# Hybrid SSD / RG-LRU layer: dt's softplus by token with sums on TensorE, no GpSimd work, output projection in two halves

## The chip, the cores and the metric

One core of a Trainium2 chip runs the whole program. The metric is the device time of one execution in microseconds. Lower is better.

## The reference

A decoder trunk of two layers on x (256 tokens, width 1024), all in float32. Each layer is a half-weighted SwiGLU FFN (width 2816), a mixer, and a second FFN. The mixer of layer 0, the hybrid, is what the change touches:

```python
z, xbc, dt_raw, gate_b, x_b = split(rms_norm(h) @ w_in)       # 1024, 1536, 16, 1024, 1024
xbc = silu(causal_dwconv(xbc)); xa, B, C = split(xbc)         # 16 heads of 64; 2 groups, state 128
dt = softplus(dt_raw + dt_bias); a = -exp(a_log)
cs = cumsum(dt * a) in chunks of 128                          # per head
y = (C B^T * exp(cs_i - cs_j), causal) @ (xa * dt)  (+ the carry of chunk 0)  + d * xa
y_a = rms_norm(y * silu(z), in two groups of 512)
xb = causal_dwconv(x_b); r, i = sigmoid(xb @ w_ra), sigmoid(xb @ w_ix)   # 16 blocks of 64
a_t = exp(-8 * r * softplus(-lambda)); h_t = a_t * h_(t-1) + sqrt(1 - a_t^2) * i * xb
y_b = gelu(gate_b) * h_t
h = h + concat(y_a, y_b) @ w_out                              # 2048 x 1024
```

## The kernel before

**Layout.** Everything is held feature-major: 128 features on the partitions, 256 tokens along the row. A float32 weight block of 1024 x 128 is split into a rounded high part (`whi`, ScalarE, L185) and the rest (`wlo`, VectorE, L190), the activations likewise (`xn`, `hid`), and a block is 24 matmuls: high by high and high by low for each of 8 tiles (L201, L202), then low by high (L205). Blocks go through a ring of four slots; SyncE loads a slot once the low part of the block four before is made, and ScalarE makes a high part once TensorE is through with the block four before.

**Phases.** FFN, hybrid, FFN, FFN, attention, FFN. In the hybrid, two blocks are a "pair": 18 pairs of the input projection (pairs 0 to 5 conv tiles of xbc, 6 to 9 of the LRU's input, 10 to 13 z, 14 to 17 gates), then 16 blocks of the output projection.

**Order.** Each engine has an order written out by hand. TensorE (`hyb_tensor`, L764) multiplies pair j and then does what `after[j]` lists: dt's product, `c_dot_b`, transposes of x to tokens (`x_to_tokens`, L795), the heads' products (`head_y`, L807/L808), the LRU's gate products (`lru_gates`, L820/L821), the group sums (one-column matmuls, L830) and their spread (L840). Before pair j it waits until pair j-2 is read out of PSUM. ScalarE (`hyb_scalar`) and VectorE (`hyb_vector`) run a loop over s: VectorE reads pair s-2 (`read_pair`, L1016), multiplies decays by C B^T (`decay_products`, L1118), makes exponents (`exponents`, L1112), makes the low parts of pair s (`convert_lo`, L190), and then does `todo[s]`, with the conv's taps of pair s-2 (L1028) last or nearly so. ScalarE makes the high parts of pair s and then does its own `todo[s]`. For pairs 15 and 16 VectorE makes the second high part too (L257).

**What the change touches.** dt's softplus is done on rows of 16 heads by 256 tokens: `softplus_args`, `softplus_u`, `softplus_ratio`, `steps_of_dt` on VectorE, `softplus_exp` and `softplus_ln` on ScalarE, then `sums_of_dt`, two scans on VectorE (L1078); TensorE turns the results into token-major columns (`rows_to_tokens`, L776), which VectorE copies to `tok`. The scanned rows `cs` also go to DRAM and come back spread over the partitions (`csb`, L751 to L756). lambda's softplus (128x8) goes along with it. GpSimd does `lru_ix` (L1252), a 128x1024 product, and `gate_y` (L1259, L1261), a product and a square of 128x512 for each two tiles. `lru_mult2`, `mult_of_lru`, `lru_scan`, `gelu`, `lru_out`, `lru_hi` and `lru_lo` make the recurrent half of `hid` (tiles 8 to 15) in steps 17 to 19 and just behind; `y_norm`, `y_hi`, `y_lo` the SSD half (tiles 0 to 7) in steps 18 and 19. `OUT_BLOCKS` (L719) orders the output blocks (tile d, half q), almost tile by tile; `out_tile` adds a finished tile to `h` and makes the next phase's input of it. The FFN before the hybrid has down pairs e = 0 to 7 with `down_out` (L614, L616) and `residual_hi` (L292).

## Time and profile before

| what | us |
|---|---|
| median of 3 runs (1081.31 to 1082.31) | 1081.52 |
| the profiled execution | 1081.11 |
| its span, first to last instruction | 1079.3 |
| TensorE busy in the span | 1054.2 |
| hybrid phase: first matmul to the next phase's first | 195.84 to 395.86 |

The profile is of one execution, and its times count from the span's start. PE is TensorE's matmuls, PEld its weight loads, DVE VectorE, ACT ScalarE, POOL GpSimd, SP SyncE. "Granted clock" is the share of 2.4 GHz that TensorE was allowed: 1.00, or 0.50, which is 1.2 GHz. Durations of neighbouring instructions overlap a little, so the time from start to start is what an instruction costs its engine.

### The profile page before, as it was taken

Reading aid. Unit: us, or ns where it says so; the run is one execution under the profiler, and the core shown is the slowest. Engines: PE = TensorE matmul, PEld = TensorE weight load, DVE = VectorE, ACT = ScalarE, POOL = GpSimd, SP = SyncE. Lnnn points to the kernel's source line nnn. Section 1 sums busy time; section 2 is a strip of 40 time slices with the busy share of each in tenths; the row PEclk is TensorE's granted clock in tenths of the full one; section 3 lists DMA queues with packets and bytes.
Section 4 is the critical chain, followed back from the end, with each engine's and each line's share of the span. In section 5 each row is a group of like instructions: output and inputs, shape, how many; then the busy total and the mean of one; then the engine's idle time right before and its main releaser. Section 6 shows DMA issues by size and latency. Waiting matters only on the chain. (4 is left out here: it accounts for less than half of the span.)

```text
span 1079.3 us, 18474 instructions
## 1 busy us (share of the span) xinstructions
PE 1054.2 (98%) x6669; PEld 949.0 (88%) x6669; DVE 807.9 (75%) x1141; ACT 614.2 (57%) x982; POOL 69.2 (6%) x80
## 2 busy tenths in 40 slices
PE   9999999998988999999999999999999999999997
PEld 8888888897888998888888888888989998888886
DVE  6888775799898758888656888766689578888753
ACT  6555543676887555555534555544455756555541
POOL 0200011100131000000011000002100000000021
PEclk9999999998988999999999999999999999999999
DMA  9866676556443656667764666775475437666671
GB/s 253 215 192 190 197 215 170 141 152 204 117 123 102 178 160 191 194 193 209 195 189 142 190 190 191 222 195 166 120 203 158 126 100 213 192 189 196 190 206 39
DMA packets 365602, 189.07 MB, mean 175 GB/s; under 512 B 5840, under 2 KB 364512, under 8 KB 365552
## 3 DMA queue, kind: packets, MB, share of 16 engines
q1 hardware_dynamic: 365296, 187.84, 61.6%
q0 software_dynamic: 256, 0.59, 0.3%
q8 instruction: 29, 0.48, 0.2%
q14 instruction: 21, 0.17, 0.1%
HBM read 186.81 MB, written 1.06 MB: 174 GB/s over the span
## 5 line engine op out<-in xcount | busy, mean ns | idle before, releaser
L190 DVE TENSOR_TENSOR wlo<-raw,whi 128x1024 fp32r<-128x1024 f32 (+1 forms) x324 | 419.8, 1315 | 67.9 <-ACT whi L185 66.3
L185 ACT ACTIVATE whi<-raw 128x1024 fp32r<-128x1024 f32 (+1 forms) x322 | 352.1, 1114 | 26.5 <-PE psum L205 19.9
L217 PE MATMUL psum<-xn,whi 128*128 128x512 f32 x1408 | 354.4, 393 | 0.1
L217 PEld LDWEIGHTS psum<-xn,whi 128*128 128x128 f32 x1408 | 253.5, 189 | 45.9 <-DVE xn L302 0.4
L220 PEld LDWEIGHTS psum<-xn,wlo 128*128 128x128 f32 x1408 | 192.4, 190 | 13.8
L220 PE MATMUL psum<-xn,wlo 128*128 128x256 f32 x1408 | 196.9, 282 | 0.0
L217 PE MATMUL psum<-hid,whi 128*128 128x512 f32 x704 | 171.8, 391 | 0.0
L217 PEld LDWEIGHTS psum<-hid,whi 128*128 128x128 f32 x704 | 128.1, 189 | 24.0
L201 PE MATMUL psum<-xn,whi 128*128 128x256 f32 x480 | 124.1, 295 | 0.7 <-ACT arena L1530 0.7
L202 PE MATMUL psum<-xn,whi 128*128 128x256 f32 x480 | 121.2, 288 | 0.0
L505 ACT ACTIVATE arena<-arena 128x256 f32<-128x256 f32 x88 | 36.9, 420 | 112.1 <-DVE arena L558 112.1
L201 PEld LDWEIGHTS psum<-xn,whi 128*128 128x128 f32 x480 | 94.8, 198 | 4.5 <-issue 3.2
L220 PEld LDWEIGHTS psum<-hid,wlo 128*128 128x128 f32 x704 | 92.9, 191 | 4.9
L202 PEld LDWEIGHTS psum<-xn,whi 128*128 128x128 f32 x480 | 94.8, 198 | 0.1
L220 PE MATMUL psum<-hid,wlo 128*128 128x256 f32 x704 | 94.4, 282 | 0.0
L292 ACT ACTIVATE xn<-h,vec 128x256 fp32r<-128x256 f32 x48 | 23.7, 506 | 116.4 <-DVE h L616 101.3
L509 ACT ACTIVATE hid<-arena 128x256 fp32r<-128x256 f32 x88 | 36.9, 419 | 88.6 <-DVE arena L563 88.6
L568 DVE TENSOR_TENSOR hid<-arena,hid 128x256 f32 (+1 forms) x88 | 37.5, 426 | 60.0 <-ACT hid L509 60.0
L205 PE MATMUL psum<-xn,wlo 128*128 128x256 f32 x480 | 68.4, 285 | 0.0
L558 DVE TENSOR_TENSOR arena<-arena,rb 128x512 f32<-128x512 f32 x88 | 60.9, 693 | 3.1
L205 PEld LDWEIGHTS psum<-xn,wlo 128*128 128x128 f32 x480 | 63.0, 195 | 0.0
L554 DVE TENSOR_TENSOR arena<-psum,arena 128x512 f32<-128x512 f32 x88 | 60.2, 684 | 3.5 <-ACT arena L500 3.5
(218 smaller groups left out, 913.6 us busy)
## 6 DMA issues: line engine op xcount, KB each, us to landing
raw<-in_ffn_gate SPq DMA_DIRECT2D x88, 512.0 KB, 3.9
raw<-in_ffn_up SPq DMA_DIRECT2D x88, 512.0 KB, 3.9
raw<-in_ffn_down SPq DMA_DIRECT2D x64, 704.0 KB, 4.6
raw<-in_hyb_w_in SPq DMA_DIRECT2D x36, 512.0 KB, 4.3
raw<-in_dif_w_qkv SPq DMA_DIRECT2D x24, 512.0 KB, 4.6
raw<-in_hyb_w_out SPq DMA_DIRECT2D x16, 512.0 KB, 4.3
raw<-in_dif_w_o SPq DMA_DIRECT2D x8, 512.0 KB, 4.3
hid<-cs_rows SPq DMA_DIRECT2D x4, 512.0 KB, 6.7
```

Source lines behind the costliest of these rows:

```text
L185: act.activation(whi[:, s, 0:k * P], raw[:, s, 0:k * P], ACT.Copy).then_inc(s_whi, 1)
L190: dve.tensor_tensor(wlo[:, s, 0:k * P], raw[:, s, 0:k * P], whi[:, s, 0:k * P].bitcast(F32), ALU.subtract).then_inc(s_wlo, 1)
L201: pe.matmul(acc, hi[:, j, :], x[:, t, 0, :], start=start and j == 0, stop=False)
L202: pe.matmul(acc, hi[:, j, :], x[:, t, 1, :], start=False, stop=False)
L205: mm = pe.matmul(acc, lo[:, j, :], x[:, k0 + j, 0, :], start=False, stop=stop and j == k - 1)
L217: pe.matmul(acc, hi[:, j, :], x[:, t, :, :], start=start and j == 0, stop=False)
L220: mm = pe.matmul(acc[:, T:2 * T], lo[:, j, :], x[:, k0 + j, 0, :], start=False, stop=stop and j == k - 1)
L505: act.activation(act_g[:, g, :], gu[:, g, 0, :], ACT.Silu).then_inc(s_silu, 1)
L509: act.activation(hid[:, bass.ds(j, 1), 0, :].rearrange("p a t -> p (a t)"), hu[:, g, :], ACT.Copy).then_inc(s_hhi, 1)
L554: dve.tensor_tensor(gu[:, g, :, :], wide_parts(g)[0], cor[:, g, :, :], ALU.add).then_inc(s_gu, 1)
L558: dve.tensor_tensor(gu[:, g, :, :], gu[:, g, :, :], rb2, ALU.mult).then_inc(s_gn, 1)
L568: dve.tensor_tensor(v[:, 1, :], hu[:, g, :], v[:, 0, :].bitcast(F32), ALU.subtract).then_inc(s_hlo, 1)
```

## The change

dt is transposed to tokens first, and softplus is done there on 128x32; the running sums are made by TensorE as products with a triangle of ones, once as rows (for `cs`) and once by token (for `tok`), and ScalarE copies them out. lambda's softplus moves into the down pairs of the FFN before. GpSimd's work moves: products to VectorE, squares to ScalarE. The masks of C B^T become one instruction for the four diagonal blocks, and ScalarE copies the other two. `x_to_tokens` uses four PSUM banks. The output projection does all eight tiles of the SSD half first, each in a bank of its own, then the recurrent half, which VectorE and ScalarE make in steps 19 to 21. The core of the diff:

```diff
 # FFN before the hybrid, ScalarE, after convert_hi of down pair e
+                    if e == 3: lambda_exp_of_lru(act)
+                    elif e == 4: lambda_ln_of_lru(act)
 # the same, VectorE, after convert_lo
+                    if e == 2: lambda_args(dve)
+                    elif e == 4: lambda_u(dve)
+                    elif e == 5: lambda_value_of_lru(dve)
...
-        OUT_BLOCKS = [(0, 0), (1, 0), (0, 1), (1, 1)] + [(d, q) for d in range(2, DT) for q in range(2)]
+        OUT_BLOCKS = [(d, q) for q in range(2) for d in range(DT)]
+        def out_sum(d):
+            return banks[(5, 7, 6, 4, 0, 1, 2, 3)[d]][:, 0:T]
-        CB_BANK = (6, 2)
+        XT_BANK = (4, 2, 5, 7)
...
 # TensorE
+            def dt_to_tokens():
+                pe.wait_ge(s_dtx, 1)
+                for c in range(TC):
+                    mm = pe.transpose(dt_tok[:, c * HEADS:(c + 1) * HEADS], dt_rows[:, c * P:(c + 1) * P],
+                                      ident[0:HEADS, 0:HEADS])
+                mm.then_inc(s_dtt, 1)
+            def sums_of_dt():
+                pe.wait_ge(s_sp, 10)
+                for c in range(TC):
+                    pe.matmul(sum_rows[:, c * P:(c + 1) * P], DTA[:, c * HEADS:(c + 1) * HEADS], tri, start=True, stop=True)
+                pe.matmul(sum_tok[:, 0:2 * HEADS], tri, DTN, start=True, stop=True)
+                pe.matmul(sum_tok[:, 2 * HEADS:], tri, DTN[:, 0:HEADS], start=True, stop=False)
+                pe.matmul(sum_tok[:, 2 * HEADS:], ones, DTA[:, 0:HEADS], start=False, stop=True).then_inc(s_sums, 1)
-            after[0] += [dt_product]
-            after[5] += [c_dot_b]
-            after[6] += [rows_to_tokens]
-            for g, s in enumerate((6, 7, 7, 8)):
+            after[0] += [dt_product, rows_of_heads]
+            after[2] += [dt_to_tokens]
+            after[5] += [sums_of_dt, c_dot_b]
+            for g, s in enumerate((6, 7, 8, 9)):
                 after[s] += [lambda g=g: x_to_tokens(g)]
-            after[14] += [lambda: group_sums(0)]
+            after[15] += [lambda: group_sums(0)]
...
 # ScalarE
+            def take_sums():
+                act.wait_ge(s_sums, 1)
+                act.activation(cs, sum_rows, ACT.Copy).then_inc(s_cs, 1)
+                act.activation(tok[:, 2 * HEADS:], sum_tok, ACT.Copy).then_inc(s_tok, 1)
+            def square_y(k):
+                act.wait_ge(s_yg, k + 1)
+                act.activation(sz[:, 2 * k:2 * k + 2, :], xbc[:, 2 * k:2 * k + 2, :], ACT.Square).then_inc(s_ysq, 1)
+            todo[3] += [softplus_exp]
+            todo[4] += [softplus_ln]
+            todo[6] += [take_sums, take_cb_off]
             for j in range(6):
-                todo[j + 3] += [lambda j=j: conv_silu(j)]
+                todo[max(j + 3, 4)] += [lambda j=j: conv_silu(j)]
-            todo[2] += [softplus_exp]
-            todo[3] += [softplus_ln]
-            todo[17] += [lambda: gelu(0), lambda: group_rms(0)]
-            todo[18] += [lambda: group_rms(1), lambda: mult_of_lru(1), lambda: gelu(1)]
-            todo[18] += [lambda: lru_hi(0)] + [lambda t=t: y_hi(t) for t in range(4)]
+            todo[15] += [lambda: square_y(0), lambda: square_y(1)]
+            todo[17] += [lambda: square_y(2), lambda: square_y(3), lambda: group_rms(0)]
+            todo[18] += [lambda: group_rms(1)] + [lambda t=t: y_hi(t) for t in range(4)]
             todo[19] += [lambda t=t: y_hi(t) for t in range(4, 8)]
-            todo[19] += [lambda: lru_hi(1), lambda: gelu(2), lambda: gelu(3)]
+            todo[19] += [lambda: mult_of_lru(1), lambda: gelu(0), lambda: gelu(1)]
+            todo[20] += [lambda: gelu(2), lambda: gelu(3), lambda: lru_hi(0), lambda: lru_hi(1)]
+            todo[21] += [lambda: lru_hi(2), lambda: lru_hi(3)]
...
 # VectorE
             def softplus_args():
+                dve.wait_ge(s_dtt, 1)
+                dve.wait_ge(s_arow, 1)
+                dve.tensor_copy(D_[:, 0:HEADS], head_rows[:, 0:HEADS]).then_inc(s_hrow, 1)
+                dve.wait_ge(s_hrow, 2)
+                dve.tensor_tensor(by_head(X_), by_head(dt_tok), D_[:, 0:HEADS].unsqueeze(1).to_broadcast([P, TC, HEADS]),
+                                  ALU.add).then_inc(s_spx, 1)
...
-            for g, s in enumerate((8, 9, 9, 10)):
+            for g, s in enumerate((8, 9, 10, 11)):
                 todo[s] += [lambda g=g: take_x(g)]
+            todo[13] += [lambda: lru_ix(0), lambda: lru_mult2(0)]
+            todo[14] += [lambda: gate_y(0), lambda: gate_y(1)]
+            todo[16] += [lambda: gate_y(2)]
+            todo[17] += [lambda: gate_y(3), lambda: y_rrms(0)]
+            todo[18] += [lambda: y_norm(0), lambda: y_rrms(1)] + [lambda t=t: y_lo(t) for t in range(4)]
+            todo[19] += [lambda: lru_ix(1), lambda: lru_mult2(1)]
+            todo[20] += [lambda: lru_scan(1), lambda: lru_out(0), lambda: lru_out(1)]
+            todo[21] += [lambda: lru_out(2), lambda: lru_out(3)] + [lambda k=k: lru_lo(k) for k in range(4)]
+            for d in range(4):
+                todo[24 + d // 2] += [lambda d=d: out_tile(d)]
+            small_work = {2: scaled_dt, 3: softplus_args, 4: softplus_u, 5: steps_of_dt}
-            for s in range(20):
+            for s in range(26):
...
-                if s == 8:
-                    take_tok()
+                if s in small_work:
+                    small_work[s]()
```

`steps_of_dt` now holds the ratio and the end of the softplus and the two products with a. In the loop `small_work` stands after `read_pair` and `decay_products` and ahead of `exponents` and `convert_lo`. The last out tiles (4 to 7) are left to the start of the next phase.

## Rows read from the trace of the kernel before

**Rows 1.** The page's first part: busy us, share of the span, instructions.

```profile
PE 1054.2 (98%) x6669; PEld 949.0 (88%) x6669; DVE 807.9 (75%) x1141; ACT 614.2 (57%) x982; POOL 69.2 (6%) x80
```

**Rows 2.** Windows of the hybrid: stretch, length, busy per engine, granted clock, DMA, GB/s.

```profile
195.80:347.40 151.60, 139.60 (x1045) 131.70 (x1044) 137.08 (x221) 113.11 (x190) 19.69 (x12) 0.93 0.51 143
347.40:395.90 48.50, 47.14 (x391) 46.83 (x391) 31.72 (x52) 25.13 (x41) 0.00 (x0) 1.00 0.54 156
```

**Rows 3.** TensorE's waits in the hybrid: us in total, times, longest.

```profile
PE psum L795 <- DVE arena L1100: 4.9, 1, 4.9
PE psum L807 <- DVE arena L1123: 4.7, 2, 2.6
PE psum L840 <- DVE small L1165: 1.6, 1, 1.6
```

**Rows 4.** Windows beside two of the holes, columns as in the second group.

```profile
303.20:306.60 3.40, 1.27 (x11) 1.08 (x10) 3.40 (x4) 3.37 (x6) 0.66 (x1) 1.00 0.10 19
306.60:310.10 3.50, 3.49 (x13) 2.71 (x14) 2.72 (x5) 2.91 (x6) 0.00 (x0) 0.51 0.99 274
337.40:344.20 6.80, 6.80 (x33) 6.80 (x33) 6.46 (x12) 4.39 (x9) 0.00 (x0) 0.50 0.54 157
```

**Rows 5.** Timeline of VectorE, steps 3 to 11: start, us, instruction, idle before.

```profile
211.74 0.69 DVE L1016 TENSOR_TENSOR arena<-psum,rb 128x512 f32<-128x512 f32 x1 [1.11 <-PE psum L205]
212.35 2.35 DVE L190 TENSOR_TENSOR wlo<-raw,whi 128x1024 fp32r<-128x1024 f32 x2
...
221.54 0.41 DVE L1055 TENSOR_TENSOR arena<-arena 16x256 f32<-16x256 f32 x1
221.99 1.74 DVE L1056 RECIPROCAL arena<-arena 16x256 f32<-16x256 f32 x1
223.77 2.46 DVE L1028 SCALAR_TENSOR_TENSOR arena<-arena,vec 128x256 f32<-128x256 f32 x6
...
247.14 0.17 DVE L1053 TENSOR_SCALAR small<-small 128x8 f32<-128x8 f32 x1
...
271.75 0.69 DVE L1016 TENSOR_TENSOR arena<-psum,rb 128x512 f32<-128x512 f32 x1
```

**Rows 6.** Timeline of VectorE, later: exponents, low parts, scans, tiles' low parts.

```profile
257.46 0.75 DVE L1112 SCALAR_TENSOR_TENSOR arena<-small,hid 128x256 f32<-128x256 f32 x2
...
300.27 2.69 DVE L1112 SCALAR_TENSOR_TENSOR arena<-small,hid 128x256 f32<-128x256 f32 x2
302.88 3.19 DVE L190 TENSOR_TENSOR wlo<-raw,whi 128x1024 fp32r<-128x1024 f32 x2
...
313.64 2.44 DVE L1141 TENSOR_TENSOR_SCAN arena<-arena 128x256 f32<-128x256 f32 x4
...
349.89 1.42 DVE L1177 TENSOR_TENSOR hid<-arena,hid 128x256 fp32r<-128x256 f32 x4
```

**Rows 7.** Timeline of ScalarE, steps 11 to 19.

```profile
273.68 0.40 ACT L913 ACTIVATE arena<-arena,small 128x128 f32<-128x128 f32 x1 [2.92 <-DVE arena L1112]
...
292.05 1.99 ACT L185 ACTIVATE whi<-raw 128x1024 fp32r<-128x1024 f32 x2
...
316.16 1.28 ACT L922 ACT_TABLE_LOAD   x1 [2.74 <-DVE arena L1141]
...
341.00 1.28 ACT L946 ACT_TABLE_LOAD   x1
342.30 0.64 ACT L946 ACTIVATE arena<-arena 128x512 f32<-128x512 f32 x1
```

**Rows 8.** Timeline of TensorE: the first group's sums, and the next phase's first matmuls.

```profile
320.24 1.84 PE L830 MATMUL psum<-con,arena 128*128 128x1 f32 x16
...
395.86 1.55 PE L217 MATMUL psum<-xn,whi 128*128 128x512 f32 x6
```

**Rows 9.** Waits of the whole execution, columns as in the third group.

```profile
ACT xn L292 <- DVE h L616: 101.3, 24, 5.3
DVE h L614 <- PE psum L220: 53.8, 24, 6.8
```

More of the change, by code:

```diff
@@ new lines, in lambda_args, with lambda_exp_of_lru, lambda_u @@
+        def lambda_args(dve):
+            dve.wait_ge(s_vec, 16)
+            dve.tensor_scalar(lt[0], vec[:, VEC["lru_lambda"]:VEC["lru_lambda"] + NL], -1.0, None,
+                              ALU.mult).then_inc(s_lmx, 1)
+        def lambda_exp_of_lru(act):
+            act.wait_ge(s_lmx, 1)
+            act.activation(lt[1], lt[0], ACT.Abs).then_inc(s_lme, 1)
+            act.wait_ge(s_lme, 1)
+            act.activation(lt[1], lt[1], ACT.Exp, scale=-1.0).then_inc(s_lme, 1)
+        def lambda_u(dve):
+            dve.wait_ge(s_lme, 2)
+            dve.tensor_scalar(lt[2], lt[1], 1.0, None, ALU.add).then_inc(s_lmu, 1)
@@ L872, in hyb_tensor @@
             for k, (d, q) in enumerate(OUT_BLOCKS):
-                if q == 0:
-                    read_out(pe, p0 + 16 + d)
+                if q == 0 and d in (4, 5):
+                    read_out(pe, p0 + 12 + d)
                 b = 2 * (p0 + 18) + k
-                multiply(pe, b, b % RING, DT, hid, 8 * q, half(p0 + 18 + d, 0), start=q == 0, stop=q == 1,
+                multiply(pe, b, b % RING, DT, hid, 8 * q, out_sum(d), start=q == 0, stop=q == 1,
                          need=ready if d == 0 else None)
@@ L993, in hyb_scalar @@
                     task()
-            for k in (2, 3):
-                lru_hi(k)
-            for s in range(20, 26):
-                convert_hi(act, p0 + s, DT)
-                residual_hi(act, n + 1, s - 20)
-            return [lambda: residual_hi(act, n + 1, DT - 2), lambda: residual_hi(act, n + 1, DT - 1)]
+            return [lambda: [residual_hi(act, n + 1, d) for d in (4, 5, 6)], lambda: residual_hi(act, n + 1, 7)]
         nlam8 = small[:, 138:146]
@@ L1124, in take_y, with lru_ix, gate_y @@
                                          ALU.add).then_inc(s_yr, 1)
+            def lru_ix(k):
+                dve.wait_ge(s_gs, 8 * k + 8)
+                dve.tensor_tensor(li[:, :, :], li[:, :, :], lxb(k), ALU.mult).then_inc(s_ix, 1)
+            def gate_y(k):
+                dve.wait_ge(s_sz, k // 2 + 1)
+                dve.wait_ge(s_yr, 2 * k + 2)
+                y = xbc[:, 2 * k:2 * k + 2, :]
+                dve.tensor_tensor(y, y, sz[:, 2 * k:2 * k + 2, :], ALU.mult).then_inc(s_yg, 1)
             def lru_mult2(k):
@@ L1178, in y_lo, with out_tile @@
                                   ALU.subtract).then_inc(s_ylo, 1)
-            todo = {s: [] for s in range(20)}
-            todo[0] += [dt_weights]
-            todo[2] += [softplus_args]
-            todo[3] += [softplus_u]
-            todo[4] += [lambda: softplus_ratio(U_, D_, M_)]
-            todo[5] += [steps_of_dt]
-            todo[6] += [sums_of_dt]
-            todo[7] += [lambda: take_cb(0), lambda: take_cb(1)]
-            for g, s in enumerate((8, 9, 9, 10)):
+            def out_tile(d):
+                dve.wait_ge(s_blk, 2 * (p0 + 18) + OUT_BLOCKS.index((d, 1)) + 1)
+                add_residual(dve, n, d, out_sum(d), 1.0)
+                residual_lo(dve, n + 1, d)
+            todo = {s: [] for s in range(26)}
+            todo[0] += [dt_weights, diagonals_of_heads]
+            todo[7] += [take_cb]
+            for g, s in enumerate((8, 9, 10, 11)):
                 todo[s] += [lambda g=g: take_x(g)]
@@ L1192, in hyb_vector @@
                 todo[10 + m] += [lambda m=m: take_y(m)]
-            todo[13] += [lambda: lru_mult2(0)]
-            todo[17] += [lambda: lru_mult2(1), lambda: lru_out(0), lambda: y_rrms(0)]
-            todo[18] += [lambda: y_norm(0), lambda: y_rrms(1), lambda: lru_scan(1), lambda: lru_out(1)]
-            todo[18] += [lambda: lru_lo(0)] + [lambda t=t: y_lo(t) for t in range(4)]
-            todo[19] += [lambda: lru_lo(1)]
+            todo[13] += [lambda: lru_ix(0), lambda: lru_mult2(0)]
[6 more added lines that the diff above has]
+            todo[21] += [lambda: lru_out(2), lambda: lru_out(3)] + [lambda k=k: lru_lo(k) for k in range(4)]
+            for d in range(4):
+                todo[24 + d // 2] += [lambda d=d: out_tile(d)]
             for j in range(10):
                 todo[j + 2] += [lambda j=j: conv_taps(j)]
-            todo[7] += [scale_of_lambda]
+            small_work = {2: scaled_dt, 3: softplus_args, 4: softplus_u, 5: steps_of_dt}
             def read_pair(j):
@@ L1208, in read_pair @@
                     gate_scaled(j - 14)
-            for s in range(20):
+            for s in range(26):
                 if s == 0:
                     before[0]()
-                if s >= 2:
+                if 2 <= s < 20:
                     read_pair(s - 2)
```

222 lines of the change are left out of this document (121 added, 101 removed).

## The prediction

> **What bounds the kernel now.** I first read the page's busy line: TensorE is busy 98% of the span [rows 1], so elsewhere there is little to win. Then the windows of the hybrid stage, up to and after the end of its 18 input pairs: 12.0 us of the first 151.6 us are idle on TensorE and its mean clock is 0.93; the output projection loses 1.4 us and keeps its clock [rows 2]. The stage ends with the first FFN matmul at 395.86 [rows 8]. TensorE's waits name the holes: 4.9 us for the take of x (L1100, itself held behind VectorE's queue), 4.7 us for `take_y` (L1123), 1.6 us for the group scale [rows 3]; with the 1.4 of the projection [rows 2] that is 12.6 us. The windows beside the holes show a second price: after 3.4 us of which TensorE was idle for 2.1, before 306.6, the clock is 0.51 for the next 3.5, and after the hole before L840 it is 0.50 for 6.8 [rows 4]. That is 1.2 GHz in place of 2.4, and half such a stretch is lost: 1.7 and 3.4 us. So over 12 us of holes and some 10 us of clock (0.07 of 151.6) are at stake. These holes all wait for VectorE, so the question is what VectorE and, through it, ScalarE still have ahead of each release.
>
> I call what VectorE and ScalarE do in the loop's round s "step s". In it VectorE reads pair s-2 and makes the low parts for pair s, which TensorE multiplies next. Prices, start to start, from VectorE's rows: read 0.61, two low parts 2.27, six taps 2.38, two exponents 0.67; a 128x512 operation 0.61, a 128x1024 one 1.13, so the 128x768 of `decay_products` 0.86; a low part of one tile 0.34, `take_y`, which also reads PSUM, 0.39 [rows 5, 6]. A pair is 48 matmuls at 0.12, 5.76 us; a block of the output projection is 2.88.
>
> **1. dt's chain (steps 2 to 7).** Removed from VectorE: 0.4 to 1.74 us operations on 16x256 (the reciprocal is 1.74 [rows 5]), two scans, three of the four `take_cb` operations, lambda's chain; together some 7 us. Added: ten operations of 128x32, bounded by 0.17 (128x8) and 0.41 (16x256), the reciprocal by 0.2 and 1.74 [rows 5]; I take 0.21 each and 0.38 for the reciprocal, near the short row since 32 is near 8: 2.3 us. But three waits come with it.
> - Step 3: the new `softplus_args` waits for the transposes that TensorE makes behind pair 2, and it stands ahead of step 3's low parts. VectorE begins step 3 when pair 1 ends, at 211.74 [rows 5]; pair 2 ends 5.76 later at 217.5, the transposes take 0.2, so its low parts begin at 218.2, where they began at 212.35. This 5.8 us is the price. TensorE barely feels it (first low part at 219.4, wanted 1.92 us into pair 3, at 219.6).
> - Step 4: ScalarE has the Ln and its reload, two `conv_silu` and their reload ahead of `conv_first`; the taps wait about 1.1 us.
> - Step 5: the ten operations stand ahead of the low parts, and pair 5 waits about 1.5 us. Step 6: `take_sums` and `take_cb_off` wait for TensorE ahead of `conv_first(4)`: 1.6 us for the taps.
>
> Steps 3 to 7 then start at 212.0, 222.9, 229.5, 237.0, 243.9; step 8 at 249.8, step 9 at 256.6, step 10 at 264.0, step 11 at 271.8. Before, step 11 started at 271.75 [rows 5]. **The 7 us saved are spent on the waits, and the gain up to step 11 is nil.** The 4.9 us hole at L795 goes, and what is late next is `take_y(0)` (VectorE at 269.4; TensorE arrives at 265.5): a new hole of about 4 us one pair later. TensorE gains 0.8 us of small matmuls (sums 0.8, two spreads 0.4, less 0.4 removed; near the 0.11 a 128-column pass takes), all of it within these holes.
>
> **2. Steps 11 to 13.** ScalarE runs without a pause from its decays at 273.68, which waited for step 11's exponents, through its reloads to the high parts of pair 13 at 292.05 [rows 7]. The start hangs on the same VectorE step, so it is equal: high part 293.1, two low parts 295.4, `take_y(3)` 295.8. That hole, one of the two at L807, stays.
>
> **3. GpSimd left out.** While GpSimd ran, the two exponents took 2.69 in place of 0.75 and the two low parts 3.19 in place of 2.35 [rows 6]. Moved to VectorE: two 128x1024 products (1.25 with their wait) and four of 128x512 (0.61); to ScalarE: four squares of 128x512 at 0.54 (the Gelu row of that shape, 0.64 busy [rows 7]). Steps 13 to 15 on VectorE: `lru_ix` 297.05; two products 299.45; read, decay, exponents 301.6; low parts 303.85; `take_y(4)` 304.3; two `gate_y` 305.45. TensorE arrives at `head_y(10)` at 304.4, where it then stood still until 306.6 [rows 4]; this hole closes, and pair 14 starts 2.65 later (two heads, four gate products, at full clock), at 307.05. Step 15: 0.61 + 0.86 + 0.67 + 3.0 (low, cast, low) = 310.6, scan 1.25 + 2.36 = 314.2, `take_y(5)` 314.7. TensorE now waits for it from 312.95: a new hole of 1.85, and 0.75 for the sigmoids behind the scan (ScalarE waits for it [rows 7]). Pair 15 starts at 318.15.
>
> Then ScalarE: sigmoids 316.95, squares 318.05, high part 319.1, sigmoids 320.5, a reload and eight lru activations 4.65 to 325.15, high parts 327.15, squares as `gate_y(3)` allows (329.5) to 330.1, reload, `group_rms(0)` 331.65, early enough for TensorE, which ends pair 16 at 332.45. The hole of 1.6 at L840 goes. Pair 17 starts at 332.45 + 0.45 + 1.75 (L830 [rows 8]) = 334.65 and ends at **340.5; before it was 347.4, where rows 2 are cut. Gain 6.9**: holes 4.5 less 2.6, clock 1.7 and 3.4.
>
> **4. The output projection.** Its total is unchanged (16 x 2.88). The first block's wait is the same chain as before (read, `y_norm`, `y_lo` of 4 tiles 1.42 [rows 6]): it ends at 345.2. But the recurrent half is now made behind it, by two engines that wait for each other: low parts 19 to 346.4; `lru_ix`, `lru_mult2` to 350.1; Sqrt 351.1; reload 1.3 and two Gelu 353.45; high parts 354.5 and 355.5; low 356.8; scan 360.4; two `lru_out` 361.6; `lru_hi(1)` 362.35; and only then ScalarE makes the high part of the seventh block: 363.4. TensorE wants the fifth at 353.85 (waits 0.65) and the seventh at 360.3 (**waits 3.15**). Blocks 7 and 8 to 369.2, the recurrent tiles are then ready (369.65, before their last one is wanted), eight blocks to 392.25. A hole of 3.15 will drop the clock, as those of 2.1 and 2.6 did: +1.7, so **393.95** against 395.86. The out tiles' residuals have 5.76 us for 5 us of work on VectorE; what ends the stage is the last tile, as before.
>
> In this part a rule speaks against the change. A reload here is 1.28 us, and the Gelu behind it starts 1.30 after it [rows 7]. The Trainium skill (ScalarE: Activation LUTs, "What ACT_TABLE_LOAD costs") gives about 1.38 us of drain beside it, 2.66 in all; by that the stage would end 1.4 us later and the gain be 0.5. The row shows no such drain, and no term here rests on it.
>
> **5. Lambda in the FFN before.** Two more reloads and four small activations on ScalarE lie in its waits for L616, 4.2 us in each down pair (101.3 by 24); on VectorE 2.1 us of 128x8 operations in one step stand beside waits of 2.2 for TensorE (53.8 by 24) [rows 9], and any rest is within the one pair's lead of the low parts. Cost nil; without that cover 0.4 us. The SyncE queue: `cs` is ready at 239.3, about 1.4 us later than before, behind weight loads which are later anyway; a broadcast that lands late for step 8 is bounded by these 1.4, and step 8 starts later too. I take nothing.
>
> **Sum.** Nil to step 11, 6.9 to the end of pair 17, then 3.3 lost in waits and 1.7 in clock: 1.9 to 2.0. The profiled execution took 1081.11 (span 1079.3); the median of the runs is 1081.52, 0.4 above it, and the difference is applied to that: **1079.5**. About 0.2% (2.2 us) is what a measurement can tell from no change, so my forecast lies on that edge.
>
> **Rivals.**
> (a) *The early chain is shorter than I think.* If ScalarE comes to `conv_first` in time in steps 4 and 6, VectorE is 2.7 earlier at step 11, and so are ScalarE's chain and everything behind it; if the waits in the output projection are also too short for the clock, 1.7 more: 1075.1. For it: the 128x32 durations are estimates. Against: each wait is an order of instructions, read in the code.
> (b) *The clock turns the gain round (slower).* New pauses lie at the ends of pairs 14 (1.85 + 0.75) and 16 (spread and sums, 2.2 us of one-column matmuls), where the clock of before fell after 2.1 idle, and for 6.8 us after 1.6 idle followed by such sums [rows 3, 4]. If they cost 1.7 and 3.4, pair 17 ends at 345.6, and the chain of part 4 hangs from that end, unshortened: 1079.5 + 5.1 = 1084.6. It decides once more than 2.0 is lost so. Against: after the same sums at 320.24, with no long hole ahead of them, the clock stayed [rows 8].
> (c) *An even result.* Step 3's wait is passed on worse than I count (a reload in front of a waiting Exp or Ln adds 1.3 on VectorE), the gain of part 3 is eaten, 1081.5.
> (d) *The slow VectorE rows were not GpSimd's doing.* Then steps 14 and 15 keep 2.8 us: 1082.3. Against: the exponents take 0.75 whenever GpSimd is still.
>
> **Numbers.** Forecast 0.50 (own range 1077.5 to 1081.5; of it 0.24 faster by over 0.2%, 0.26 within), (a) 0.20, (b) 0.16, (c) 0.10, (d) 0.04, of which half within. Faster 0.44, same 0.38, slower 0.18. Range 1074.8 to 1085.0, from (a) to (b).
>
> **What would show it.** Step 3 of VectorE: its low parts begin at about 218, after a wait for TensorE of 5 to 6 us; step 11 begins within 1 us of 271.8. No wait of L795's kind, one of about 4 us for the first `take_y`. No VectorE exponents above 0.8. Pair 17 ends near 340.5. One hole of about 3 us at the seventh output block, which waits for its high part. First FFN matmul after the stage near 394. Wrong if step 11 begins 3 us earlier, or if the seventh block finds its high part ready.

## The result, and the profile after

| what | before | changed |
|---|---|---|
| median, us | 1081.46 (12 runs) | 1083.49 (12 runs, 1083.21 to 1085.57) |
| ratio to before | | 1.0024 [1.0016, 1.0031] |
| the profiled execution, us | 1081.11 | 1083.84 |
| its span, us | 1079.3 | 1082.0 |
| pair 17's last matmul ends | 347.6 | 342.5 |
| first FFN matmul after the hybrid | 395.86 | 397.92 |

The change makes the kernel slower by 0.2%. The forecast, 1079.5, was 4.0 us too low and on the wrong side. Ratios, here and below, leave out the slow executions, which are one of e5 (1721 us) and one of the kernel before beside it (2650 us). By the first part of the profile's page (compare [rows 1]) the changed kernel has 9 us less work on VectorE and 18 us less on GpSimd, and it gains nothing from that:

```profile
PE 1054.6 (97%) x6678; PEld 948.0 (88%) x6678; DVE 798.7 (74%) x1140; ACT 616.3 (57%) x989; POOL 51.1 (5%) x70
```

The windows up to and after the end of pair 17 (columns as in [rows 2]) show where it went: the input pairs are 4.9 us shorter, the output projection 6.9 us longer, at a clock of 0.94 where it was 1.00. TensorE's idle time in the two windows together is 15.8 us, where it was 13.4 [rows 2]. That is the loss. TensorE's busy time fell by 0.4 us, and over both windows the clock was low for less time than before (13.6 us, where it was 20.5).

```profile
195.80:342.50 146.70, 136.11 (x1057) 127.74 (x1056) 116.78 (x196) 107.96 (x186) 1.59 (x2) 0.98 0.53 148
342.50:397.90 55.40, 50.18 (x388) 49.28 (x388) 40.06 (x64) 28.36 (x47) 0.00 (x0) 0.94 0.48 134
```

The window of before is cut 0.2 us ahead of pair 17's end. By one and the same event, TensorE's first matmul of the output projection, the gain up to there is 5.1 us. The first line is of the kernel before, the second of the changed one:

```profile
347.81 0.36 PE L201 MATMUL psum<-hid,whi 128*128 128x256 f32 x1
342.68 0.36 PE L201 MATMUL psum<-hid,whi 128*128 128x256 f32 x1
```

TensorE's waits in the hybrid (us in total, times, longest; compare [rows 3]). L914 is the wait of `head_y` for `take_y`; L201 for ScalarE's high parts is the fifth block (0.50) and the seventh (2.82); L217 is the FFN's first block.

```profile
PE psum L914 <- DVE arena L1224: 7.8, 4, 3.9
PE psum L201 <- ACT whi L185: 3.3, 2, 2.8
PE psum L201 <- DVE hid L1289: 1.4, 1, 1.4
PE psum L205 <- DVE wlo L190: 1.2, 1, 1.2
PE psum L928 <- ACT arena L1038: 0.9, 1, 0.9
PE psum L217 <- issue: 0.6, 1, 0.6
```

Windows of the changed kernel around the two stretches of low clock in the hybrid (columns as in [rows 2]). One begins at 269.3, in the hole for the first `take_y`, which ends at 270.43; one at 364.9, in the seventh block's hole, which ends at 365.64. Each is 6.8 us long. What lies in the hole costs nothing, so half of the rest is the price: at most 2.9 and 3.1 us.

```profile
272.50:276.50 4.00, 4.00 (x14) 3.30 (x13) 4.00 (x7) 2.01 (x7) 0.00 (x0) 0.54 0.17 49
...
366.00:368.30 2.30, 2.30 (x12) 2.30 (x12) 2.30 (x3) 0.54 (x1) 0.00 (x0) 0.50 0.06 18
368.30:371.80 3.50, 3.50 (x19) 3.50 (x18) 3.50 (x11) 3.18 (x7) 0.00 (x0) 0.51 0.94 263
371.80:375.00 3.20, 3.20 (x29) 3.20 (x29) 3.20 (x4) 1.66 (x3) 0.00 (x0) 1.00 0.28 79
```

VectorE's timeline (columns as in [rows 5]) in steps 3, 5, 11 and 14. Step 3's low parts begin at 218.49 behind a wait of 5.29 for the transposes; step 5 starts at 229.84, and behind its read come dt's ten operations, which take 2.3 us; step 11 starts at 272.56; and the two exponents cost 0.75 in step 14 too, where [rows 6] had 2.69.

```profile
218.18 0.17 DVE L1166 COPY arena<-psum 128x16 f32<-128x16 f32 x1 [5.29 <-PE psum L869]
218.39 0.19 DVE L1168 TENSOR_TENSOR arena<-psum,arena 128x32 f32<-128x32 f32 x1
218.49 2.35 DVE L190 TENSOR_TENSOR wlo<-raw,whi 128x1024 fp32r<-128x1024 f32 x2
...
230.44 0.17 DVE L774 TENSOR_SCALAR arena<-arena 128x32 f32<-128x32 f32 x1
...
231.09 0.35 DVE L777 RECIPROCAL arena<-arena 128x32 f32<-128x32 f32 x1
...
232.71 2.35 DVE L190 TENSOR_TENSOR wlo<-raw,whi 128x1024 fp32r<-128x1024 f32 x2
...
272.56 0.70 DVE L1129 TENSOR_TENSOR arena<-psum,rb 128x512 f32<-128x512 f32 x1
...
302.53 0.75 DVE L1210 SCALAR_TENSOR_TENSOR arena<-small,hid 128x256 f32<-128x256 f32 x2
```

ScalarE's timeline in the projection shows the seventh block's high part (the L185 at 364.55) behind the recurrent half (L1070 is `lru_hi`), which itself waited 4.63 us for VectorE's scan and products.

```profile
353.29 1.28 ACT L1061 ACT_TABLE_LOAD   x1
354.59 1.15 ACT L1061 ACTIVATE arena<-arena 128x512 f32<-128x512 f32 x2
...
363.31 1.33 ACT L1070 ACTIVATE hid<-arena 128x256 fp32r<-128x256 f32 x4 [4.63 <-DVE arena L1265]
364.55 1.99 ACT L185 ACTIVATE whi<-raw 128x1024 fp32r<-128x1024 f32 x2
...
396.78 1.99 ACT L185 ACTIVATE whi<-raw 128x1024 fp32r<-128x1024 f32 x2
```

VectorE's timeline at the end of the projection shows the out tiles (L427 adds a tile to the residual, L302 makes its low part, L364 adds its squares). One tile takes 1.81 us, 0.66 of it idle, because the low part waits for ScalarE's high part of the tile just added. Tile 6 is the last ahead of the FFN's first weights, whose high parts ScalarE therefore starts only at 396.78 (fence above).

```profile
391.98 0.42 DVE L427 SCALAR_TENSOR_TENSOR h<-psum,h 128x256 f32<-128x256 f32 x1
393.05 0.48 DVE L302 SCALAR_TENSOR_TENSOR xn<-h,vec,xn 128x256 fp32r<-128x256 f32 x1 [0.65 <-ACT xn L292]
393.45 0.42 DVE L364 TENSOR_TENSOR sumsq<-sumsq,sq 128x256 f32<-128x256 f32 x1
393.79 0.42 DVE L427 SCALAR_TENSOR_TENSOR h<-psum,h 128x256 f32<-128x256 f32 x1
```

### The profile page after: what moved, and what is told of

Its sections match the earlier page's. It is cut to its first block and busy times, and to the rows that moved or that the text cites. A ratio compares the mean times of both kernels' runs of the same rounds, so it can differ in the third digit from the quotient of the medians.

```text
span 1082.0 us, 18485 instructions
## 1 busy us (share of the span) xinstructions
PE 1054.6 (97%) x6678; PEld 948.0 (88%) x6678; DVE 798.7 (74%) x1140; ACT 616.3 (57%) x989; POOL 51.1 (5%) x70
## 5 line engine op out<-in xcount | busy, mean ns | idle before, releaser
L185 ACT ACTIVATE whi<-raw 128x1024 fp32r<-128x1024 f32 (+1 forms) x322 | 351.3, 1113 | 21.8 <-PE psum L205 15.2
L217 PE MATMUL psum<-xn,whi 128*128 128x512 f32 x1408 | 354.5, 393 | 0.7 <-issue 0.6
L217 PEld LDWEIGHTS psum<-xn,whi 128*128 128x128 f32 x1408 | 253.5, 189 | 46.9 <-issue 1.0
L217 PE MATMUL psum<-hid,whi 128*128 128x512 f32 x704 | 171.8, 391 | 0.0
L217 PEld LDWEIGHTS psum<-hid,whi 128*128 128x128 f32 x704 | 128.1, 189 | 24.1
L201 PE MATMUL psum<-xn,whi 128*128 128x256 f32 x480 | 121.0, 290 | 1.4 <-ACT arena L1610 0.7
L202 PE MATMUL psum<-xn,whi 128*128 128x256 f32 x480 | 117.8, 283 | 0.0
L201 PEld LDWEIGHTS psum<-xn,whi 128*128 128x128 f32 x480 | 92.0, 192 | 4.8 <-issue 2.7
L202 PEld LDWEIGHTS psum<-xn,whi 128*128 128x128 f32 x480 | 92.1, 192 | 0.2
```

Of the source, the lines that this page charges most:

```text
L185: act.activation(whi[:, s, 0:k * P], raw[:, s, 0:k * P], ACT.Copy).then_inc(s_whi, 1)
L201: pe.matmul(acc, hi[:, j, :], x[:, t, 0, :], start=start and j == 0, stop=False)
L202: pe.matmul(acc, hi[:, j, :], x[:, t, 1, :], start=False, stop=False)
L217: pe.matmul(acc, hi[:, j, :], x[:, t, :, :], start=start and j == 0, stop=False)
```

## The experiments

Each ratio is to the kernel before on the same chip, from 5 to 12 executions; the changed kernel's is 1.0024. "Pair 17 ends" and "FFN" (the first FFN matmul) are times of the one profiled execution. "Low clock" lists its stretches of 1.2 GHz in the hybrid, start and length. The hybrid phase itself begins at 195.96 in the changed kernel and anywhere from 195.21 (e7) to 196.35 (e5) in the others, though no edit touches what stands ahead of it. So a time of one profile is uncertain by about half a us before an edit has done anything.

| run | ratio | pair 17 ends | FFN | low clock |
|---|---|---|---|---|
| changed kernel | 1.0024 [1.0016, 1.0031] | 342.5 | 397.92 | 269.3/6.8, 364.9/6.8 |
| e1 args late | 1.0009 [0.9999, 1.0018] | 341.7 | 397.04 | 268.4/3.4, 316.2/3.4, 364.0/6.8 |
| e3 high parts ahead | 1.0006 [0.9997, 1.0015] | 342.0 | 394.97 | 268.8/6.8, 395.1/3.4 |
| e4 GpSimd back | 1.0028 [1.0018, 1.0038] | 346.2 | 399.44 | 269.9/6.8, 307.4/6.8, 331.3/3.4, 368.8/3.4 |
| e5 halves undone | 1.0014 [1.0005, 1.0023] | 343.0 | 398.06 | 270.2/6.8, 348.7/6.8 |
| e7 hole filled | 1.0026 [1.0015, 1.0038] | 340.9 | 395.68 | 270.6/3.4, 396.9/3.4 |
| e8 tiles early | 1.0015 [1.0006, 1.0023] | 342.3 | 397.69 | 269.3/6.8, 364.9/6.8 |
| e9 = e3 + e8 | 1.0003 [0.9994, 1.0012] | 342.2 | 394.79 | 269.0/6.8, 395.3/3.4 |
| e10 = e9 + early chain | 0.9973 [0.9963, 0.9984] | 339.4 | 391.88 | 292.9/3.4, 313.4/3.4, 391.9/3.4 |
| e11 = e10 + overlap | 0.9936 [0.9922, 0.9949] | 339.3 | 390.18 | 266.5/6.8 |
| e12 = e3 + overlap | 0.9959 [0.9946, 0.9973] | 342.4 | 392.36 | 269.3/6.8 |
| e13 overlap alone | 0.9994 [0.9985, 1.0004] | 342.8 | 396.06 | 269.9/6.8, 365.5/3.4 |
| e14 = e12 + GpSimd back | 0.9978 [0.9969, 0.9987] | 343.6 | 392.16 | 270.7/3.4, 308.2/3.4, 328.7/3.4 |

**Step 3's wait.** `softplus_args` to the end of step 3, the Exp behind the taps' first sums:

```diff
-small_work = {2: scaled_dt, 3: softplus_args, 4: softplus_u, 5: steps_of_dt}
+todo[3] += [softplus_args]
+small_work = {2: scaled_dt, 4: softplus_u, 5: steps_of_dt}
```

> One part of the changed kernel moved: softplus_args stands at the end of VectorE's step 3 and softplus_exp behind conv_first(1) on ScalarE. The changed kernel has VectorE idle for 5.3 us in step 3. Theory A (the early chain is what VectorE loses, and it is passed on to the end): step 4 starts 4.6 us earlier, the taps of steps 4 and 6 then wait for ScalarE 2 us or more each, step 11 starts about 2.4 us earlier (270.1) and the time is 1081.0, 2.4 under the changed kernel's 1083.5. Rival B (the early half is covered by TensorE's and ScalarE's own chain from step 11 on): step 11 is earlier, but pair 17 still ends at 342.5, time 1083.5 within 0.5.

The low parts of step 3 began at 212.76 and pair 5's wait fell from 1.24 to 0.57. Step 11 began at 270.85 in place of 272.56, 1.7 us earlier, and pair 17 ended 0.8 earlier, with one more stretch of low clock on the way (316.2). So most of the 5.3 us wait was slack, or was taken up again by the waits behind it. The ratio fell by 0.0015, 1.6 us, more than these 0.8. Neither expectation is met in full.

**The seventh block's hole.** The first two recurrent high parts go behind the high parts of blocks 7 and 8 on ScalarE:

```diff
-todo[20] += [..., lambda: lru_hi(0), lambda: lru_hi(1)]
-todo[21] += [lambda: lru_hi(2), lambda: lru_hi(3)]
+todo[21] += [lambda k=k: lru_hi(k) for k in range(4)]
```

> One part of the changed kernel moved: ScalarE makes the high parts of output blocks 7 and 8 ahead of lru_hi(0) and lru_hi(1). Theory A (the loss is made in the output projection, where the seventh block waits for ScalarE behind the recurrent tiles and the clock falls to 0.50 for 6.8 us after it): the hole of 2.8 us and the 3.4 us lost at the low clock go, first FFN matmul at about 391.7 in place of 397.9, time 1077.3. Rival B (TensorE would only wait elsewhere, for the recurrent tiles at the ninth block): the hole moves there, 3 us, with the same clock, time 1083.0 to 1083.5.

TensorE's waits from 342 to 395.5 in this run:

```profile
PE psum L217 <- issue: 2.8, 1, 2.8
PE psum L201 <- DVE hid L1289: 1.4, 1, 1.4
PE psum L201 <- ACT whi L185: 0.5, 1, 0.5
PE psum L205 <- DVE wlo L190: 0.3, 1, 0.3
```

The hole and the low clock behind it are gone, and the blocks end at 392.14 in place of 397.36. But 2.84 us of it come back as a wait of the FFN's first block, with a low clock of its own. From the end of pair 17 on, the blocks take 4.8 us less, 2.3 of it go into that wait, and the low clock behind it costs up to 1.7 more. The rival expected such a wait, but at the ninth block. The prediction has no such limit.

**The clock alone.** 26 matmuls of no use ahead of the seventh block, so that TensorE doesn't stand still there (its output is left alone):

```diff
 b = 2 * (p0 + 18) + k
+if k == 6:
+    for _ in range(26):
+        pe.matmul(banks[3][:, T:2 * T], xn[:, 0, 0, 0:P], xn[:, 0, 0, :], start=True, stop=True)
```

> The changed kernel with 26 matmuls of 256 columns (about 3.1 us, into an unused half of a bank, result not used) put ahead of the seventh output block, where TensorE stands still for 2.8 us. Nothing waits for them. Theory A (half of the loss there is the clock that falls behind the hole): the clock stays at 1.00, the block starts at most 0.3 us later, and the time falls by 3.1 to 3.4 us, to 1080.2. Rival B (the low clock costs nothing, because the blocks behind it wait for VectorE and ScalarE anyway): time 1083.5 to 1083.8.

The clock stayed at 1.00, and the blocks ended at 393.18, 4.2 earlier. Of this, 1.6 is not the edit's: the hybrid began 0.75 earlier, and the first stretch was 3.4 and not 6.8. The edit gained the other 2.6. The FFN's first block then waited 2.51 in place of 0.57, and the clock fell there for 3.4 us. By this profile these two cost 1.9 and 1.7 and take back all of it and more, and the median did not move. So the low clock behind the seventh block does have a price (2.6 us here, where theory A has 3.1 to 3.4), and the limit just behind it hides it. (The profiled execution took 1082.46, 1.2 below this kernel's median.)

**GpSimd.** The two `lru_ix` and the four `gate_y` with their squares back on GpSimd:

```diff
-todo[13] += [lambda: lru_ix(0), lambda: lru_mult2(0)]
-todo[14] += [lambda: gate_y(0), lambda: gate_y(1)]
+todo[13] += [lambda: lru_mult2(0)]
...
+def hyb_gpsimd(pool, n):
...
+    lru_ix(0)
+    for k in range(3):
+        gate_y(k)
+    lru_ix(1)
+    gate_y(3)
...
```

> The changed kernel with lru_ix and gate_y (product and square) on GpSimd as before; all else as changed. Theory A (GpSimd slows VectorE while it runs, and leaving it out gains): the exponents of step 14 take 2.7 again and the low parts 3.2, a hole of about 2 us opens ahead of pair 13's heads or pair 14, pair 17 ends 2 to 5 us later, and the time is 1085.5 to 1088. Rival B (the 5 us of products that VectorE took over cost as much as the slowing): the time stays within 0.7 of 1083.5. Rival C: it falls by 2 us or more, to 1081.5, since the chain of the recurrent half in the output projection loses the 1.3 us of lru_ix(1).

VectorE's slow rows came back with it, at the same places and of the same length as in [rows 6]:

```profile
302.04 2.70 DVE L1209 SCALAR_TENSOR_TENSOR arena<-small,hid 128x256 f32<-128x256 f32 x2
304.66 3.19 DVE L190 TENSOR_TENSOR wlo<-raw,whi 128x1024 fp32r<-128x1024 f32 x2
```

So rival (d) is out. VectorE's read of a pair, which has one input in PSUM, kept its 0.68 beside GpSimd (start 299.95). The Trainium skill (SBUF — State Buffer, "SBUF: two separate sides") says that a VectorE operation with two inputs in SBUF and a GpSimd operation that reads SBUF hold a shared pair of ports exclusively, one blocking the other; these rows agree with it. Pair 17 ended 3.7 later, but the FFN began only 1.5 later, since the seventh block then waited 2.20 with a low stretch of 3.4 in place of 2.82 with one of 6.8. The ratio moved by 0.0004. Theory A had the mechanism, rival B the time.

**The order of the blocks.** The old order of the blocks, the recurrent half in steps 17 to 19, one out tile a step:

```diff
-OUT_BLOCKS = [(d, q) for q in range(2) for d in range(DT)]
+OUT_BLOCKS = [(0, 0), (1, 0), (0, 1), (1, 1)] + [(d, q) for d in range(2, DT) for q in range(2)]
...
```

> The changed kernel with the order of the output blocks of before, the recurrent half made in steps 17 to 19 and just behind, and the out tiles one in each step as before; dt's chain and GpSimd as changed. Theory A (what costs is not the order of the blocks but that VectorE now makes the recurrent half alone, wherever that stands): the wait for the second half of the first output block's tiles grows from 1.4 to some 6 us, the clock falls behind it, and the time is 1083 to 1086. Rival B (the halves are what lost the gain): TensorE ends the stage as before or earlier, 1078 to 1081.

The waits for `hid` were 5.9 us in two (3.96 and 1.94), the clock fell once for 6.8, and the FFN began at 398.06. Halves or pairs of blocks come out alike here; the 0.0010 between the two ratios is within their intervals. The two kernels differ in one more thing: in e5 a block's low parts stand between a tile's add and its low part, and its FFN did not wait. So this run alone does not price the order of the blocks.

**The out tiles.** First only earlier: tiles 0 to 3 one behind each of the last four blocks' low parts. Then with e3's edit. Then also with dt's chain out of the way (e1's edit, `steps_of_dt` behind step 5's low parts, `conv_first(2)` and `(4)` ahead of the Ln and of `take_sums`).

```diff
-todo[24 + d // 2] += [lambda d=d: out_tile(d)]
+between = before[1] if s == 0 else (lambda s=s: out_tile(2 * (s - 24))) if s >= 24 else lambda: None
+convert_lo(dve, p0 + s, DT, s in ROUNDED_BY_VECTOR, between)
+if s >= 24:
+    out_tile(2 * (s - 24) + 1)
```

> The changed kernel with out tiles 0 to 3 put between the conversions of the last four output blocks on VectorE and ScalarE, one tile behind each block, in place of two behind each pair of blocks. The runs with the seventh block's wait taken away or filled both ended the projection 4 to 5 us earlier and then stood still for 2.5 to 2.8 us at the FFN's first block, since VectorE and ScalarE need 1.8 us for a tile and start the first one only when the last but two block is converted. Theory A (this chain of tiles is a third limit just behind the others): alone it gives only the 0.6 us that TensorE waits there now, 1082.9, with the 2.8 us hole and the low clock still there. Rival B (the tiles are no limit of their own, the FFN's first weights are): no change, the wait at the FFN's first block stays.

> Both parts together: high parts of output blocks 7 and 8 ahead of lru_hi, and out tiles 0 to 3 one behind each block. Theory A (the two are limits one behind the other): no hole at the seventh block, no low clock, and no wait above 0.5 us at the FFN's first block, which starts at about 392.2 in place of 397.9; time 5.7 under the changed kernel, about 1077.8. Rival B (TensorE then waits for another thing before the FFN, the last tile or its weights, for 2 us or more): 1081.5, as with the first part alone.

> The kernel of e9_ahead_and_tiles with dt's chain re-ordered too: softplus_args at the end of step 3, steps_of_dt behind the low parts of step 5, conv_first(2) and conv_first(4) first in ScalarE's steps 4 and 6. Theory A (VectorE's waits in steps 3, 4 and 6, 5.3, 1.05 and 2.05 us in the changed kernel, are what kept the first half from gaining): step 11 starts at 267 to 269 in place of 272.6, pair 17 ends 3 to 5 us before 342.5, time 3 to 5 below e9, about 1074. Rival B (from step 11 on TensorE's own work of 8.5 us for each pair with gates sets the pace): step 11 is earlier but pair 17 ends no more than 1.5 us earlier, time 1076.5 or more.

e8 left the holes where they were. In e9 the tiles began 2.5 us earlier than in e3 (376.87), and it was of no use: each then took 3.39 us together with its block, tiles 4 to 6 took 1.81 each as before, and the FFN's block still waited 2.52, as the rival expected. So the start of the tiles is not the limit; their pitch, the time from one tile's start to the next one's, is the candidate, and the next runs test it. e10 moved pair 17 by another 2.8 and the FFN by 2.9, and is the first version that beats the kernel before. The blocks' wait at the FFN stayed (2.39).

**The pitch of the out tiles.** VectorE adds tile 5 before it makes tile 4's low part, and tile 6 before tile 5's; e12 and e13 do this for tiles 0 to 3 too.

```diff
-return [lambda: [out_tile(d) for d in (4, 5, 6)], lambda: out_tile(7)]
+def last_tiles():
+    out_add(4); out_add(5); out_lo(4)
+    out_add(6); out_lo(5); out_lo(6)
+return [last_tiles, lambda: out_tile(7)]
```

> e10_early_chain_too with one more edit: at the end of the hybrid stage VectorE adds out tiles 4 and 5 before it makes tile 4's low part, and tile 6 before tile 5's, so that it no longer stands still for ScalarE's high part in each tile (0.66 and 0.99 us of waits of each 1.81 us in e10). Theory A (the chain of out tiles is what holds the FFN's first weights): ScalarE has tile 6's high part at about 388.0 where e10 had it at 390.02, the FFN's first block is converted about 2.0 earlier, its first matmul is at about 389.8 where e10 had 391.88, the wait of 2.39 there falls to 0.3 and the low clock at 391.9 (3.4 us of 1.2 GHz, 1.7 lost) goes: 3.8 us in all, ratio about 0.9938 (e10 0.9973). Rival B (the weights' DMA or a free slot of the ring is what ScalarE waits for as soon as the tiles are out of its way): first FFN matmul 391.2 or later, a wait named DMA raw on ScalarE, clock still low, ratio 0.9968 or more.

> The changed kernel with two small edits in the output projection alone: lru_hi(0), (1) behind the high parts of blocks 7 and 8 (as in e3_hi_ahead), and the out tiles' adds one ahead of their low parts (tiles 0 and 1, 2 and 3, 4 to 6). dt's chain and GpSimd stay as changed. Theory A (what the changed kernel lost is in the projection's two chains): the hole at the seventh block is gone as in e3; seven tiles cost VectorE about 1.15 us each in place of 1.81, the FFN's first weights are ready at about 391.7, TensorE ends its blocks at 392.14, first FFN matmul about 392.3 (e3 394.97), no low clock at 395: 4.4 us under e3, ratio about 0.9965, so faster than the kernel before. Rival B (the loads into the ring or the end of the kernel's own clock eat it): first FFN matmul 394 or later, or it is at 392.5 and the median does not follow; ratio 0.9990 or more.

> The changed kernel with the overlap of the out tiles alone (VectorE adds tile d+1 before it makes tile d's low part), lru_hi where the change put it. Theory A (two limits stand one behind the other, and each hides the other's gain): the seventh block still waits about 2.8 us and the low clock at 364.9 stays, TensorE ends its blocks at 397.36 as in the changed kernel, and only the 0.57 us of wait at the FFN's first block can go: first FFN matmul about 397.5, ratio about 1.0019. With e3_hi_ahead's -0.0018 and the two together at -0.0065, the pair is worth more than the sum of its parts. Rival B (the overlap is worth its 4 us by itself, e3's edit added little): ratio 0.9985 or less.

VectorE's timeline in e12, and its window from the end of pair 17 to the FFN:

```profile
387.95 0.75 DVE L427 SCALAR_TENSOR_TENSOR h<-psum,h 128x256 f32<-128x256 f32 x2
389.02 0.48 DVE L302 SCALAR_TENSOR_TENSOR xn<-h,vec,xn 128x256 fp32r<-128x256 f32 x1 [0.33 <-ACT xn L292]
389.43 0.41 DVE L364 TENSOR_TENSOR sumsq<-sumsq,sq 128x256 f32<-128x256 f32 x1
389.76 0.41 DVE L427 SCALAR_TENSOR_TENSOR h<-psum,h 128x256 f32<-128x256 f32 x1
390.10 0.47 DVE L302 SCALAR_TENSOR_TENSOR xn<-h,vec,xn 128x256 fp32r<-128x256 f32 x1
```

```profile
342.40:392.40 50.00, 47.83 (x390) 46.84 (x389) 39.95 (x64) 28.36 (x47) 0.00 (x0) 1.00 0.52 148
```

The waits of the low parts for ScalarE are gone but for 0.33 in one of two. Tiles 4 to 6 take 3.6 us where they took 5.4, the FFN's weights are ready when the blocks end, and the projection takes 50.0 us at full clock in place of 55.4. With these two small edits (e12) the changed kernel goes from 1.0024 to 0.9959, and with the early chain to **0.9936**. e11's first FFN matmul came within 0.4 of what was expected (0.79 of wait stayed, with the clock at 1.00).

e13 was a miss in size. Its hole at the seventh block was the same 2.82, but the clock behind it fell for 3.4 us and not for 6.8. Its FFN is 1.86 us earlier: 1.6 is that clock, 0.57 is the wait, which alone is the edit's by its mechanism, and pair 17's later end takes 0.3 off. The ratio, from 12 executions, is lower by 0.0030 nevertheless, 3.2 us. The executions fall into two groups: seven of 1078.8 to 1079.7 us with a mean granted clock of 0.993 to 0.997, and five of 1081.1 to 1082.7, the profiled one among them, with 0.991 to 0.993. So more than half of them are better than what the profile shows, and their clock is no lower; at which hole they gain it is open. Together with e3 (-0.0018) this makes -0.0048, against -0.0065 for both in one kernel; the intervals don't exclude that the two simply add.

**GpSimd without the other limits.** e12 with e4's edit:

> e12_ahead_overlapped (both limits of the projection mended, ratio 0.9959) with GpSimd given back its products and squares, as in e4_gpsimd_back. There pair 17 ended 3.7 us later than in the changed kernel, but the kernel was only 0.0004 slower. Theory A (the gain of leaving GpSimd out is real, and in the changed kernel it is lost behind the projection's limits and in the clock): pair 17 ends at about 346.1 again against 342.41 in e12, the first FFN matmul is 3 to 4.5 us later than e12's, ratio 0.9985 to 1.0000. Rival B (VectorE has slack there, and the end hangs from something else than pair 17): first FFN matmul less than 1.5 us later than in e12, ratio 0.9973 or less.

It fell between the two expectations: 0.0019 slower than e12, some 2 us, with intervals that overlap by 0.0004. By the profile it is no slower, but its hybrid began 0.6 us earlier than e12's; counted from there its FFN is 0.4 later and its pair 17 ends 1.8 later. Its windows, and after them e4's at the same place in the same code, show why one profile can't settle it: TensorE stands still for the same `take_y`, and the clock is low for 3.4 us in the one (it is 1.00 again from 311.80) and for 6.8 in the other.

```profile
308.30:311.80 3.50, 3.50 (x13) 2.97 (x12) 3.46 (x6) 3.47 (x8) 0.00 (x0) 0.53 0.68 179
311.80:315.00 3.20, 3.20 (x29) 3.20 (x29) 3.17 (x5) 1.21 (x2) 0.00 (x0) 1.00 1.03 288
```

```profile
307.40:310.80 3.40, 2.42 (x10) 1.89 (x11) 2.97 (x6) 3.16 (x4) 0.00 (x0) 0.50 0.85 211
310.80:314.20 3.40, 3.40 (x11) 2.75 (x11) 3.37 (x5) 3.37 (x8) 0.00 (x0) 0.52 0.59 154
```

The three stretches of e14 lose 5.1 us. The three of e4 up to pair 17 are 17.1 us long, and some 7.5 us are lost there, since 2.0 us of them lie in holes; the code is the same up to there. By the medians, leaving GpSimd out is worth about 2 us once the projection lets it through, though with intervals that overlap this is not clear of the noise. In the changed kernel as it was it is 0.4, less than can be told from nothing. How much of pair 17's 3.7 us in e4 was its own and how much the clock's stays open.

## Why the prediction was wrong

**What bounds the kernel; step 3 to step 11 (part 1).** The mechanism is right, the size a little off. Low parts of step 3 at 218.49 (218.2 predicted); the taps of steps 4 and 6 waited 1.05 and 2.05 (1.1 and 1.6); pair 5 waited 1.24, with 0.69 more ahead of it (1.5); the ten operations took 2.3; step 11 began at 272.56 (271.8). L795's hole went and one of 3.87 came at the first `take_y` (4). "The gain up to step 11 is nil" was a loss of 0.8 us, most of it from step 6, where the taps waited longer. That this part could give more is shown by e10: with the same work in another order pair 17 ends 2.8 us earlier.

**Steps 11 to 13 (part 2): the first step that failed.** "The start hangs on the same VectorE step, so it is equal." It was not equal. Pair 13's high parts came at 293.59, where they had been at 292.05 [rows 7], and `take_y(3)` ended at 297.34, not at 295.8. Of these 1.54 us, 0.8 is step 11's later start. The other 0.7 is the clock: the new hole at the first `take_y` came with 6.8 us of low clock, to which the sum gave no cost, TensorE ended pair 10 late, and ScalarE waited for it ahead of the second of pair 12's high parts.

```profile
281.79 1.06 ACT L185 ACTIVATE whi<-raw 128x1024 fp32r<-128x1024 f32 x1 [0.61 <-PE psum L205]
293.59 1.99 ACT L185 ACTIVATE whi<-raw 128x1024 fp32r<-128x1024 f32 x2
```

The same code shows this in two lengths. In e1, e7 and e14, where that stretch was 3.4 us, it is 20.3 us from the start of step 11 to these high parts, as in the kernel before; in the changed kernel, e3, e5, e8, e9, e12 and e13, where it was 6.8, it is 20.9 to 21.2. The kernel before had 6.8 us of low clock behind its own hole (252.0 to 258.9), but that lay well ahead of step 11, which started without a wait for TensorE.

**GpSimd left out (part 3).** The mechanism is shown, by the exponents at 0.75 and by e4. From the end of `take_y(3)` to the end of pair 17 it took 45.0 us (44.7 predicted). The holes fell otherwise than predicted: the one for `take_y(3)`, which was to stay at 2.6, was 0.59, and the next, which was to close, was 1.62. The gain up to the end of pair 17 was 5.1 and not 6.9. (The 347.4 of the prediction is 0.2 ahead of that pair's last matmul's end.)

**The output projection (part 4): the second step.** The holes were sized well: fifth block 0.50 (0.65), seventh 2.82 (3.15). The clock's term, "+1.7", was too small: the ten blocks behind the hole took 31.7 us, where at 2.88 each they are 28.8, so 2.9 in this execution. Behind the same hole in e13 they took 30.1, 1.3 more than at full clock. And "the out tiles' residuals have 5.76 us for 5 us of work on VectorE; what ends the stage is the last tile, as before" counted VectorE's work and not its waits for ScalarE between an add and its low part. A tile's work is 1.15 us and its pitch 1.81. In the changed kernel that chain cost only 0.57 at the FFN's first block, because the late blocks hid it; in e3 it cost 2.84 and the clock. It is the reason why mending the known hole alone gave so little: the FFN began 2.95 us earlier, the blocks had ended 5.2 earlier.

Together, of the 4.0 us by which the FFN came late (397.92 against 393.95): 1.8 up to the end of pair 17 (0.8 in dt's chain, 0.7 from the clock, 0.3 behind them), 0.4 from there to the seventh block, 1.2 of clock behind that, 0.57 at the FFN. So about half is clock and half is waits. The two spans differ by 2.7, the FFN's starts by 2.06. Of the 0.6 between them, 0.5 lies at the end of the kernel, where in the changed one the clock had fallen already (1.22 us for TensorE's last products in place of 0.71).

**The rule on the reload.** The Gelu starts 1.30 after a reload of 1.28 (353.29 to 354.59), so the drain of about 1.38 us that the Trainium skill puts beside it (ScalarE: Activation LUTs, "What ACT_TABLE_LOAD costs") is not to be seen here either; it is no part of the loss.

**The rivals.** (a) did not occur, but e10 shows that its 2.7 us were there to be had. (b), the clock, at 1084.6, is nearest to the 1083.49 measured, but that is in part luck. Its places, the ends of pairs 14 and 16, were wrong: the clock stayed there and fell at the first `take_y` and in the projection. And by itself the clock cost 1.9 us more than forecast, just short of the 2.0 with which (b) was to decide; the waits made up the rest. It had been given 0.16, and the forecast's own range had no clock in it but one stretch of 3.4. (c) is excluded by the interval as a result, though the direction of its first part is there in the 0.8 us of dt's chain. (d) is excluded by e4. On part 5, lambda and the SyncE queue, there is no test: the hybrid begins 0.12 us later than before, less than the scatter between profiles.

## What to carry to other kernels

Where two engines make a tile in turns (add, high part, low part), its price is the pitch with both waits and not one engine's work; add the next tile before the low part of this one. When a hole is closed, read which chain ends next behind it: here the out tiles took back 2.3 of the 4.8 us that the seventh block gained, and two edits together gave 7 us where the first alone gave 2. In an estimate, charge a hole of 2 to 4 us with its clock at the longer of the lengths that the traces show, also where the pairs seem to have slack. In the profiled hybrids of this case 28 of 29 holes of over 2 us came with a low stretch; the exception is the 2.22 us at the first `take_y` of e10.

## What the runs showed that I had not expected

The length of a low-clock stretch is not set by the size of the hole. Behind the same hole of 2.82 us it was 6.8 us in the changed kernel, e1 and e8, and 3.4 in e13; at the first `take_y`, behind holes of 3.85 to 3.87, it was 6.8 in the changed kernel and seven of the others, 3.4 in e1, e7 and e14. What goes with the length is the moment at which the clock fell. In 15 of the 33 stretches, from the hybrids of all fourteen profiles to the FFN's first block, it fell while TensorE still had 0.64 us or more to stand, and all 15 are 6.8 us long (in one of them, e5's at 348.6, a wait of 1.94 was just about to begin). In the other 18 it fell at most 0.55 us before TensorE went on, or behind that; 17 of these are 3.4 us long, and one is 6.8 (337.4 in the kernel before, during the one-column sums). This is read from the traces; no run was made to test it. And a low stretch needs no hole: in e4 (331.2) and e14 (328.7) TensorE had not waited, but had just done the 16 one-column matmuls of the group's sums.

So a single profile is uncertain by 1.7 us a hole. The profiled execution lay above its kernel's median by 0.3 us in the changed kernel, 0.9 in e12 and 1.5 in e11 and e13, and below it by 0.9 in e14 and 1.2 in e7.

GpSimd's effect on VectorE is large and repeats: step 14's two exponents took 2.69 or 2.70 beside it in the kernel before, e4 and e14, and 0.75 without it.
